# Page look-up of the expert indices split between VectorE, GpSimd and ScalarE, and twelve expert items moved from one stage to another

## The reference, cut to what matters

```
qry = (xi @ w_query).reshape(PEER_BLOCK, PEER_HEADS, 2, PEER_HALF)
s = jnp.einsum('thpc,pnc->thpn', qry, sub_keys)
s1, i1 = lax.top_k(s[:, :, 0], PEER_TOPK)      # the 16 best first keys
s2, i2 = lax.top_k(s[:, :, 1], PEER_TOPK)      # the 16 best second keys
cand = s1[..., :, None] + s2[..., None, :]     # 256 sums
cidx = i1[..., :, None] * PEER_KEYS + i2[..., None, :]
top_s, pos = lax.top_k(cand, PEER_TOPK)        # the 16 best sums
idx = jnp.take_along_axis(cidx, pos, axis=-1)  # the experts' numbers
gate = jax.nn.softmax(top_s, axis=-1)
hid = gelu(einsum('td,thkd->thk', xi, expert_u[idx]))
return einsum('thk,thkd->td', gate * hid, expert_v[idx])
```

## Time and profile before

| | us |
|---|---|
| median of 3 runs | 4448.75 (4448.02 to 4449.22) |
| the profiled execution | 4443.61 |
| its span on the core | 4441.8 |
| DVE busy in the span | 3311.2 (75%) |
| PE busy | 2360.4 (53%) |
| POOL busy | 2273.9 (51%) |
| ACT busy | 583.7 (13%) |

### The profile page before, as it was taken

The page is one execution under the profiler, slowest core; times in us unless marked ns, Lnnn a source line. Parts: engine busy times, 40 slices in busy tenths (PEclk is TensorE's granted clock), DMA queues, the critical chain, the costliest instruction groups (busy, mean ns, idle before and its releaser), DMA issues. The chain is left out here.

```text
span 4441.8 us, 35225 instructions
## 1 busy us (share of the span) xinstructions
PE 2360.4 (53%) x11697; PEld 1871.1 (42%) x11697; DVE 3311.2 (75%) x4373; ACT 583.7 (13%) x1447; POOL 2273.9 (51%) x1217
## 2 busy tenths in 40 slices
PE   6999999998489999989749774100000000000000
PEld 5888888777466666666537553000000000000000
DVE  2333232305889999989877888999998899999998
ACT  2222222301112222222210011000000000000000
POOL 1001001000245555555565511888887888888886
PEclk8999999999789999999969887555555555555555
DMA  6766666486789999999999964999999999999998
GB/s 174 224 205 208 195 195 200 138 312 228 255 346 407 406 414 411 408 378 403 372 375 410 398 250 155 406 422 422 417 422 396 401 423 422 419 418 419 408 422 350
DMA packets 444577, 1513.70 MB, mean 341 GB/s; under 512 B 42688, under 2 KB 276852, under 8 KB 278492
## 3 DMA queue, kind: packets, MB, share of 16 engines
q0 software_dynamic: 161840, 1158.85, 64.2%
q1 hardware_dynamic: 269880, 251.94, 17.8%
q10 hardware_dynamic: 12672, 100.67, 5.7%
HBM read 1384.96 MB, written 126.21 MB: 340 GB/s over the span
## 5 line engine op out<-in xcount | busy, mean ns | idle before, releaser
L1962 DVE SCALAR_TENSOR_TENSOR ex_y<-ex_ring,ex_wt,ex_y 128x2048 f32<-128x2048 f32 x538 | 1265.3, 2352 | 96.2 <-DMA ex_ring<-in_peer_v_dram,idx_all 47.0
L1947 DVE CUSTOM_DVE_ANT_0 ex_ring<-ex_ring,ex_xi 128x2048 f32<-128x2048 f32 x544 | 1244.0, 2289 | 122.6 <-DMA ex_ring<-in_peer_u_dram,ex_idx_s 51.1
L1869 POOL DMA_INDIRECT ex_ring<-in_peer_u_dram,idx_all x384 | 791.6, 2062 | 313.3 <-DVE ex_hid L1947 209.7
L1869 POOL DMA_INDIRECT ex_ring<-in_peer_v_dram,idx_all x384 | 757.6, 1973 | 234.9 <-DVE ex_y L1962 116.9
L1901 PE MATMUL ex_fold<-ex_y,const 128*32 128x512 f32 (+1 forms) x48 | 24.4, 670 | 1111.9 <-DVE ex_y L1962 1111.9
L870 PE MATMUL heads_b_pj<-xnT_b,lead 128*128 128x304 f32 x2048 | 599.0, 430 | 15.5 <-DVE mixT_b L1539 9.4
L1901 PEld LDWEIGHTS ex_fold<-ex_y,const 128*32 128x32 f32 (+1 forms) x48 | 6.2, 135 | 1129.5 <-DVE ex_y L1962 1113.2
L1869 POOL DMA_INDIRECT ex_ring<-in_peer_v_dram,ex_idx_s x160 | 290.8, 1817 | 275.5 <-DVE ex_y L1962 186.8
L1869 POOL DMA_INDIRECT ex_ring<-in_peer_u_dram,ex_idx_s x160 | 322.8, 2017 | 203.8 <-DVE ex_hid L1947 159.6
L870 PEld LDWEIGHTS heads_b_pj<-xnT_b,lead 128*128 128x128 f32 x2048 | 371.9, 194 | 126.3 <-issue 13.7
L870 PE MATMUL heads_a_pj<-xnT_a,heads_a_w 128*128 128x256 f32 x1216 | 315.9, 397 | 1.7 <-DMA heads_a_w<-in_w_in_dram 1.7
(11 more groups left out here) (584 smaller groups left out, 3967.0 us busy)
## 6 DMA issues: line engine op xcount, KB each, us to landing
lead<-w_scratch SPq DMA_DIRECT2D x64, 1024.0 KB
heads_a_w<-in_w_in_dram SPq DMA_DIRECT2D x38, 1024.0 KB, 6.0
w_scratch<-heads_a_w ACTq DMA_DIRECT2D x38, 1024.0 KB, 4.2
lead<-in_w_in_dram SPq DMA_DIRECT2D x26, 1024.0 KB, 5.9
w_scratch<-lead ACTq DMA_DIRECT2D x26, 1024.0 KB, 4.2
out_a_w<-in_w_out_dram SPq DMA_DIRECT2D x7, 2048.0 KB, 14.4
w_out_scratch<-out_a_w ACTq DMA_DIRECT2D x7, 2048.0 KB, 9.4
out_b_w<-w_out_scratch SPq DMA_DIRECT2D x7, 2048.0 KB, 12.8
```

What stands on the lines that cost most here:

```text
L1869: pool.indirect_dma_start(self.ring[:, i % RING, :], None, self.tables[which], bass.IndirectOffsetOnAxis(ap=self.index(s, g, k), axis=0)). ...
L1947: nc.vector.tensor_tensor_reduce(ring, ring, self.tokens(s)[:], 1.0, 0.0, ALU.mult, ALU.add, self.hid[:, g % 2, k:k + 1]).then_inc(self.se ...
L1962: nc.vector.scalar_tensor_tensor(y, ring, wt, y, ALU.mult, ALU.add).then_inc(self.sem["consumed"], 1)
```

## The change

Three things. `OVERLAP` takes 318 items among group b's heads where it took 330, and 48 in its routing where it took 36. In both routings the products and the sums of the look-up go from DVE to POOL: DVE does both comparisons one behind the other into a tile that is twice as large, and signals `marked`; POOL multiplies both, and adds them as a tree (the two lists' halves together, the seventeenth column to the first, then 8, 4, 2 columns, then the last pair). ACT multiplies the first list's table by 128 beforehand, and copies the sum to `idx_all` as an integer. And POOL's gathers stand in its list between these: those of step 4h+3 ahead of the products, those of step 4h+4 between products and adds.

```diff
-OVERLAP = {"norm": 14, "heads": 330, "out": 48, "ffn": 8, "route": 36}
+OVERLAP = {"norm": 14, "heads": 318, "out": 48, "ffn": 8, "route": 48}
...
+    def gather_to(self, pool, step):
+
+        if self.stream:
+            self.stream.gather(pool, self.at(step))
...
-         "hot": ([P, T, TOPK, TOPK + 1],), "pick": ([P, 2, T, TOPK],),
+         "hot": ([P, 2, T, TOPK, TOPK + 1],), "pick": ([P, 2, T, TOPK],),
...
+            def index(h):
+
+                n = len(tiles_of(h))
+                act.wait_ge(sem["picked"], h + 1)
+                nc.scalar.copy(mem["idx_all"][:, group.slot:group.slot + n, h, :], B.pick[:, h % 2, 0:n]).then_inc(sem["indexed"], 1)
...
+                if h >= 1:
+                    index(h - 1)
...
-                nc.scalar.copy(B.table[:, 0, 0:T, 0:1], B.at[:, 0:T, 0, 0:1])
-                nc.scalar.copy(B.table[:, 0, 0:T, 1:], B.at[:, 0:T, 0, :])
+                nc.scalar.mul(B.table[:, 0, 0:T, 0:1], B.at[:, 0:T, 0, 0:1], float(KEYS))
+                nc.scalar.mul(B.table[:, 0, 0:T, 1:], B.at[:, 0:T, 0, :], float(KEYS))
...
+            index(HEADS - 1)
...
-                dve.wait_ge(sem["tabled"], h + 1)
+                if h >= 1:
+                    dve.wait_ge(sem["picked"], h)
                 for s in range(2):
                     n = TOPK + 1 - s
-                    hot, shape = B.hot[:, 0:T, :, 0:n], [P, T, TOPK, n]
-                    order.link(nc.vector.tensor_tensor(
-                        hot, B.place[:, s, 0:T].unsqueeze(3).to_broadcast(shape),
-                        cst("iota", 0, n).unsqueeze(1).unsqueeze(1).to_broadcast(shape), ALU.is_equal))
-                    order.link(nc.vector.tensor_tensor(
-                        hot, hot, B.table[:, s, 0:T, 0:n].unsqueeze(2).to_broadcast(shape), ALU.mult))
-                    order.link(nc.vector.tensor_reduce(B.pick[:, s, 0:T], hot, AX_X, ALU.add))
-                dve.sem_inc(sem["picked"], 1)
-                order.mark(nc.vector.scalar_tensor_tensor(mem["idx_all"][:, own, h, :], B.pick[:, 0, 0:T], float(KEYS),
-                                                          B.pick[:, 1, 0:T], ALU.mult, ALU.add))
+                    shape = [P, T, TOPK, n]
+                    last = nc.vector.tensor_tensor(
+                        B.hot[:, s, 0:T, :, 0:n], B.place[:, s, 0:T].unsqueeze(3).to_broadcast(shape),
+                        cst("iota", 0, n).unsqueeze(1).unsqueeze(1).to_broadcast(shape), ALU.is_equal)
+                last.then_inc(sem["marked"], 1)
...
-            dve.sem_inc(sem["routed"], 1)
...
+            for h in range(HEADS):
+                T = len(tiles_of(h))
+                order = Counter(pool, sem["pool_order"], h, 10)
+                share.gather_to(pool, h * PARTS + 3)
+                pool.wait_ge(sem["marked"], h + 1)
+                pool.wait_ge(sem["tabled"], h + 1)
+                hot = [B.hot[:, s, 0:T] for s in range(2)]
+                for s in range(2):
+                    n = TOPK + 1 - s
+                    order.mark(nc.gpsimd.tensor_tensor(
+                        hot[s][:, :, :, 0:n], hot[s][:, :, :, 0:n],
+                        B.table[:, s, 0:T, 0:n].unsqueeze(2).to_broadcast([P, T, TOPK, n]), ALU.mult))
+                share.gather_to(pool, h * PARTS + 4)
+                order.wait()
+                order.link(nc.gpsimd.tensor_tensor(hot[0][:, :, :, 0:TOPK], hot[0][:, :, :, 0:TOPK], hot[1][:, :, :, 0:TOPK],
+                                                   ALU.add))
+                order.link(nc.gpsimd.tensor_tensor(hot[0][:, :, :, 0:1], hot[0][:, :, :, 0:1], hot[0][:, :, :, TOPK:], ALU.add))
+                for n in (8, 4, 2):
+                    order.link(nc.gpsimd.tensor_tensor(hot[0][:, :, :, 0:n], hot[0][:, :, :, 0:n], hot[0][:, :, :, n:2 * n], ALU.add))
+                if h >= 2:
+                    pool.wait_ge(sem["indexed"], h - 1)
+                nc.gpsimd.tensor_tensor(B.pick[:, h % 2, 0:T].unsqueeze(3), hot[0][:, :, :, 0:1], hot[0][:, :, :, 1:2], ALU.add
+                                        ).then_inc(sem["picked"], 1)
+                order.close()
             share.gather(pool)
             if group is LATER:
-                pool.wait_ge(sem["routed"], 1)
+                pool.wait_ge(sem["indexed"], HEADS)
```

More of the change, by code:

```diff
@@ L2188, in route @@
         "w_in0 w_in1 w_in2 w_in3 w_packed0 w_packed1 w_packed2 w_packed3 projected0 projected1 query_copied0 query_copied1 scored0 scored1 scores_copied0 scores_copied1 "
-        "scores_read cleared dve_passed dve_order tabled picked best_found negated exped routed",
+        "scores_read cleared dve_passed dve_order tabled marked picked indexed pool_order best_found negated exped",
         {"w": ([P, 2, KT, P],), "q": ([P, 2, N],), "q_fold": ([P, 2, P],), "sc": ([P, T, 2, KEYS],), "top": ([P, T, 2, TOPK],),
```

## The result

The changed kernel takes 4457.64 us (median of 15 runs, 4450.58 to 4466.08), the kernel before 4447.60 beside it (15 runs, 4438.78 to 4459.11): a ratio of 1.0023, 95% interval 1.0016 to 1.0030, so 10 us slower. That is just past the line of 0.2% that the prediction drew; it had 4456, in the range of 4430 to 4475.

What follows compares the result with a forecast made beforehand. DVE and transfers were taken to pace the later heads, with PE close behind, and DVE's own sequence the last routing. Terms -25 + 27.8 - 30.6 + 22 + 9 + 7 - 3 gave +7.2 us: median 4456, range 4430 to 4475.

Steps and rivals of the forecast that it cites:

- step 1: Later group's heads: twelve items fewer relieve DVE and the transfers, -25 us (bounds 0 and -28).
- step 7: First routing: DVE's look-up shrinks but PE sets the pace and the last look-up ends later, -3 us (-5 to +1).
- rival C: Later group's heads: PE sets the pace, so fewer items save 0 to 10 us; 4471 to 4481, chance 0.10.
- Step 4: Last routing: POOL's products hold DVE's gate product and the item behind it, +22 us (0 to +34).
- Rival A: Last routing: DVE is not held by POOL's products, sum -15 us, 4434; chance 0.22.
- rival B: Last routing: POOL's adds hold DVE too, or its instructions are dearer; hold 34 us, 4468, chance 0.16.
- Step 5: Last routing: item 416's wait for the first set's sum to leave grows, +9 us (4 to 12).
- Step 6: End of the last routing: the last head's adds and ACT's copy delay what follows, +7 us (4 to 10).
- Step 3: Last routing: look-up products and sums leave DVE in eight heads, -30.6 us.
- step 2: Last routing: twelve items more cost DVE +27.8 us, their transfers fitting under the DMA share.
- Rival D: Last routing: the moved work all comes back as waiting through shared ports, 30.6 us for 22; 4464, chance 0.08.

Runs made afterwards that it cites:

- e1: The kernel before with only the quotas changed to 318 and 48, look-up left on DVE: 4472.53 us, ratio 1.0052.
- e8: The changed kernel with the first routing's whole look-up left on DVE: 4470.61 us, ratio 1.0049.
- e2: The changed kernel with the old quotas 330 and 36, so only the look-up's products and sums move: 4434.86 us, ratio 0.9968.
- e3: The changed kernel with POOL's two products moved behind the gathers of step 4h+4, next to the adds: 4454.76 us, ratio 1.0015.
- e7: The changed kernel with the look-up of the last routing's last head made on DVE: 4458.05 us, ratio 1.0030.
- e9: The changed kernel with eight more POOL adds at the end of the last routing's last head: 4473.08 us, ratio 1.0057.
- e4: The changed kernel with POOL's look-up work behind step 4h+5's gathers and each routing's last head looked up on DVE: 4438.40 us, ratio 0.9978.
- e5: The kernel of e4 with the old quotas 330 and 36: 4424.24 us, ratio 0.9943.
- e6: The kernel of e4 with 342 items among the heads and 24 in the last routing: 4447.35 us, ratio 1.0002.

## Why the prediction was right, and where it was not

The time was right, within 2 us of the forecast (as a difference, +10.0 for +7.2), and the last routing, on which most of the argument stood, came out at +33.4 for +35. But two steps were mis-sized against each other: step 1 promised 14 us that did not come, step 7 left out 5 that did. That the sum came so close is in part luck. The outcome that I gave most weight, no change, rests on a line of 0.2%; the measured 0.23% lies just past it, and the 15 runs of the kernel before spread over 20 us, where I had put their scatter at 0.03%.

**Step 1** is the wrong one. "DVE's 94% busy share scales 27.8 to 26. I take -25": the heads gave 11 in this trace and about 10 in all (the three traces with 330 items have 1048.6, 1050.7 and 1052.9 us, the seven with 318 lie between 1037.5 and 1044.3, with a mean of 1040.5). A busy share of 94% doesn't say that the engine sets the pace. DVE's busy time did fall by the 27 us, as the heads' window of before beside that of after shows:

```profile
1255.00:2304.00 1049.00, 900.12 (x4304) 653.46 (x4304) 972.94 (x1095) 265.94 (x585) 581.20 (x327) 0.93 0.97 394
```

972.9 fell to 945.7, but the stage by 11, so DVE idles 16 us more. Where, the longest waits of DVE among the heads tell (us in total, times, longest), before and after:

```profile
DVE heads_b_pmax L1600 <- PE heads_b_F L1142: 11.8, 13, 3.5
DVE ex_y L1958 <- DMA out_y_prompt_dram<-ex_y: 11.4, 1, 11.4
DVE ex_ring L1947 <- DMA ex_ring<-in_peer_u_dram,idx_all: 10.0, 8, 2.0
DVE ex_ring L1947 <- DMA ex_ring<-in_peer_u_dram,ex_idx_s: 9.8, 2, 8.3
```

```profile
DVE heads_b_pmax L1600 <- PE heads_b_F L1142: 15.1, 11, 3.4
DVE ex_y L1958 <- DMA out_y_prompt_dram<-ex_y: 13.0, 1, 13.0
DVE heads_b_vN L1506 <- PE heads_b_R L991: 12.2, 8, 2.4
DVE heads_b_f_qkvT L1561 <- ACT heads_b_f_root L1294: 7.4, 4, 2.8
DVE heads_b_ors L1534 <- ACT heads_b_ort L1270: 6.1, 8, 2.6
```

The waits for items' transfers make room for waits for PE and ACT: all DVE's waits for PE there are 19.8 us before and 38.9 after, for ACT 9.8 and 21.6, for DMA 35.8 and 21.5. Of the last, 11.4 and 13.0 are one wait for a sum's transfer (L1958), so those for items are 24.4 and 8.5. With 306 items they grow on:

```profile
DVE heads_b_pmax L1600 <- PE heads_b_F L1142: 22.8, 14, 3.4
DVE heads_b_vN L1506 <- PE heads_b_R L991: 18.6, 11, 4.1
```

So the items had filled gaps that DVE has anyway while the next product is made. I had put that as rival C and gave it 0.10; its number (0 to -10 for -25) is about what held. Its mechanism held by half: DVE does wait for PE, but also more for ACT, and PE is not shown at its limit. PE is idle for 149 us of this stage before and 143 after, and waits for DVE in 115 and 111 of them. The engines wait for each other in turn. e1 shows it in the time: the quotas alone cost 25 us, where my terms 1 and 2 and the 4.5 us of term 5 that the place of item 416 alone gives would have made it 7.

**Step 7** was too small: -7.9 for -3. All traces agree: from the first search to the next stage the first routing takes 132.7 to 133.1 us in the three with the look-up on DVE (before, e1, e8), and 125.1 in the five where all of it is on POOL (after, e2, e3, e7, e9). With the look-up gone from DVE the matmuls follow each other without a pause, where PE waited 1.55 us a head:

```profile
1112.85 1.34 PE L2268 MATMUL route_a_ps<-skT,route_a_q 128*128 128x128 f32 x8
...
1127.84 1.34 PE L2268 MATMUL route_a_ps<-skT,route_a_q 128*128 128x128 f32 x8
```

A head takes 1127.84 - 1112.85 = 14.99 us where it took 16.53, the low end of the 15 to 16 that I had: 7 x 1.54 = 10.8 less. The first head, which I had left out, is 3.4 us shorter too (12.64 us from its first search to its gate product, for 16.06), and the end gives back 6.4, more than my 3 to 4: from the last gate product to the next stage it is 7.7 for 1.3.

**Step 4** was right in mechanism, and a little large: 18.4 us for 22, mainly since the products take 2.41 and 3.45 us a head for the 2.58 and 3.88 that I scaled. e3 shows that the hold belongs to the instructions with two operands in SBUF, and that the search is not held. That is what the Trainium skill says in "SBUF — State Buffer", section "Who interferes with whom": a DVE instruction with at most one input in SBUF, outside the two-port modes, doesn't contend with GpSimd. Rival A (no hold) is out. The adds of rival B hold nothing in the changed kernel, where the search covers them; in e3 and e4 they hold the candidate sums. The hold goes both ways: in e4 an add of 48 elements on POOL takes 2.25 us, where 0.33 is its time, when it meets an item (DVE's from 2590.13 to 2593.71):

```profile
2586.27 3.45 POOL L2431 TENSOR_TENSOR route_b_hot<-route_b_hot,route_b_table 128x816 f32<-128x816 f32 x2
2589.80 1.83 POOL L2435 TENSOR_TENSOR route_b_hot<-route_b_hot 128x768 f32<-128x768 f32 x1
2591.71 2.25 POOL L2437 TENSOR_TENSOR route_b_hot<-route_b_hot 128x48 f32<-128x48 f32 x1
```

**Step 5**, +9: 9.7. **Step 6**, +7: 6.7, and e9 shows that it goes through to the end. In e1 and e2, however, item 416's wait came out 2 to 5 us above the same reckoning, as the first of the two transfers takes 9.6 and 10.7 us there, for 7.5; step 5 took it as fixed. In the changed kernel it took 8.5. What makes it longer is not shown.

**Step 3**, -30.6, and **step 2**, +27.8: together with steps 4 to 6 they had +35 and made 33.4. In e1 the twelve items cost 30.3.

Rival D, that the moved work comes all back as waiting, is nearly true of the last routing as it was written (in e2, -1 us), but not by its mechanism: in e2 the holds give back 16.5 us of the 30.6, the late end 6.3 and item 416's wait 6.7. e4 and e5 take most of the holds and the late end away, and with the old quotas (e5) the last routing is then 15.6 us shorter than before (232.4 for 248.0).

## What to carry to other kernels

A busy share close to one on an engine is no proof that less work there shortens the stage: vary the work by a few per cent both ways and read the slope, and look at what the engine waits for afterwards. Work that goes from DVE to POOL is worth what it costs beside instructions that don't share the ports: put it beside those, and look at what stands behind it in POOL's list (transfers that others wait for, the end of the stage). An edit of two parts is measured in its parts: here one was worth -13 us and the other cost 25, and the first with most of the holds and the late end taken away gives -22.

## What the runs showed of the hardware that was not expected

- The price of an item among the heads is not even: 0.9 to 1.3 us each between 306 and 330 items, 3.6 from 330 to 342 (single traces).
- POOL's products with a repeated operand take 2.41 us for 544 + 512 elements, 2.3 ns for an element; an add of 32 elements takes 0.25 us, so the fixed part of that is below 0.25.
- The first of the two transfers of a sum, with an add in the memory, took 7.5 us before, 10.7 in e2 and 20.3 in e6, where it was issued right behind four gathers.
